# A fused two-block network on one core: the taps of a state-space batch, the phases and the attention steps placed anew

## The reference, cut to what matters

```
proj = h @ w_in[l]                       # 2048 x 6144: u, z_s, q, k, v, z_a
u, z_s, q, k, v, z_a = split(proj)
# state-space mixer: 64 groups of 16 channels, 64 complex states each
a_bar = exp(lam * step);  b_bar = ((a_bar - 1) / lam) * b_mat
bu = einsum('gnp,bsgp->bsgn', b_bar, u)
states = associative_scan(x_t = a_bar * x_(t-1) + bu_t)
y = einsum('gpn,bsgn->bsgp', c_mat, states).real + d_skip * u
y = gelu(y);  ab = y @ w_glu + b_glu;  y_s = ab[:1024] * sigmoid(ab[1024:]) * silu(z_s)
# differential attention: 8 heads of 2 maps, causal
w = softmax(q0 k0) - lam * softmax(q1 k1);  o = rms_norm(w @ v, sub_g) * (1 - lambda_init)
y_a = o * silu(z_a)
x = x + gate * (concat(y_s, y_a) @ w_out[l])
```

## Time and profile before

| what | value |
|---|---|
| median of three runs | 3105.74 us |
| the profiled execution | 3101.39 us |
| its span on the core | 3099.6 us |
| TensorE matmul, busy | 2911.4 us (94%) |
| VectorE, busy | 2148.8 us (69%) |
| ScalarE, busy | 1535.5 us (50%) |
| GpSimd, busy | 284.4 us (9%) |
| mean granted share of TensorE's clock | 0.976 |

### The profile page before, as it was taken

One profiled execution on the slowest core, in us unless ns is written; L12 is line 12 of the kernel. 1 busy time (PEld: TensorE's weight loads), 2 busy tenths in 40 slices (PEclk: granted clock), 3 DMA queues, 4 the chain that ended last, 5 costly groups with the idle time before them and its releaser, 6 DMA issues.

```text
span 3099.6 us, 59134 instructions
## 1 busy us (share of the span) xinstructions
PE 2911.4 (94%) x24112; PEld 2695.1 (87%) x24112; DVE 2148.8 (69%) x3498; ACT 1535.5 (50%) x2404; POOL 284.4 (9%) x488
## 2 busy tenths in 40 slices
PE   6899999998999999999999999999899999999987
PEld 2578777788988889999888888999899999999987
DVE  6367777687788877766665667675888746887465
ACT  3335555365555655644343434545555544555454
POOL 0012212100122220200000010010000000000000
PEclk9899999998999999999999999999999999999999
DMA  9887776884645455554333334555455555555543
GB/s 376 309 264 256 248 266 232 286 287 158 179 153 164 155 182 194 177 181 157 107 108 110 115 117 137 163 178 184 134 190 185 186 184 180 181 187 177 184 151 116
DMA packets 168223, 580.91 MB, mean 187 GB/s; under 512 B 40272, under 2 KB 40304, under 8 KB 155536
## 3 DMA queue, kind: packets, MB, share of 16 engines
q1 hardware_dynamic: 146784, 525.40, 51.1%
q0 software_dynamic: 20592, 48.26, 5.1%
q10 hardware_dynamic: 576, 3.47, 0.3%
HBM read 555.22 MB, written 21.76 MB: 186 GB/s over the span
## 4 chain that ended last, share of the span: by engine, by line
PE 68%; DVE 15%; DMA 7%; ACT 5%; issue 4%; SPq 1%; POOL 0%; DVEq 0%; ACTq 0%
PE acc L988 67%; DVE arena L948 6%; ACT arena L985 3%; DVE upper L948 2%; DVE arena L958 1%; DMA arena<-in_w_ada 1%; DMA arena<-scr_k 1%; DVE rounded L941 1%; DMA arena<-in_w_in 1%; DMA scr_k<-arena 1%; DVE upper L958 1%; PE acc L991 1%; DMA upper<-in_w_ada 1%; ACT L985 1%; ACT upper L985 1%
## 5 line engine op out<-in xcount | busy, mean ns | idle before, releaser
L988 PE MATMUL acc<-rounded 128*128 128x256 f32 x14688 | 1913.1, 289 | 33.4 <-issue 14.3
L988 PEld LDWEIGHTS acc<-rounded 128*128 128x128 f32 x14688 | 1820.8, 194 | 117.1 <-issue 88.0
L944 ACT ACTIVATE rounded<-arena 128x1024 fp32r<-128x1024 f32 x802 | 847.7, 1059 | 735.4 <-PE acc L988 554.5
L941 DVE TENSOR_TENSOR rounded<-arena,rounded 128x1024 fp32r<-128x1024 f32 x802 | 974.8, 1225 | 247.0 <-ACT rounded L944 246.7
L988 PEld LDWEIGHTS acc<-upper_rounded,rounded 128*128 128x128 f32 x4560 | 551.8, 193 | 16.2 <-issue 14.0
L988 PE MATMUL acc<-upper_rounded,rounded 128*128 128x256 f32 x4560 | 557.7, 284 | 1.4 <-DVE rounded L941 0.9
L985 ACT ACTIVATE arena<-arena 128x256 f32<-128x256 f32 (+4 forms) x477 | 251.3, 527 | 226.3 <-DVE arena L948 143.1
L948 DVE TENSOR_TENSOR arena<-arena 128x256 f32<-128x256 f32 (+5 forms) x458 | 244.0, 533 | 46.2 <-ACT arena L985 33.2
L948 DVE TENSOR_TENSOR arena<-acc,arena 128x256 f32<-128x256 f32 (+4 forms) x270 | 117.2, 434 | 222.7 <-PE acc L988 213.2
L988 PE MATMUL acc<-arena 128*32 128x512 f32 (+8 forms) x1550 | 214.5, 487 | 51.4 <-DVE arena L948 23.0
L958 DVE SCALAR_TENSOR_TENSOR arena<-arena 128x256 f32<-128x256 f32 (+6 forms) x465 | 208.1, 448 | 51.0 <-ACT arena L985 35.3
(11 more groups left out here) (94 smaller groups left out, 1260.2 us busy)
## 6 DMA issues: line engine op xcount, KB each, us to landing
arena<-in_w_in SPq DMA_DIRECT2D x328, 512.0 KB, 4.6
arena<-in_w_ada SPq DMA_DIRECT2D x88, 1024.0 KB, 5.4
arena<-in_w_up SPq DMA_DIRECT2D x176, 512.0 KB, 4.1
arena<-in_w_down SPq DMA_DIRECT2D x88, 512.0 KB, 3.9
arena<-in_w_outa SPq DMA_DIRECT2D x32, 512.0 KB, 6.7
arena<-in_w_glu SPq DMA_DIRECT2D x32, 512.0 KB, 6.2
arena<-in_w_outm SPq DMA_DIRECT2D x32, 512.0 KB, 4.6
arena<-in_w_out SPq DMA_DIRECT2D x32, 512.0 KB, 4.3
```

Source lines behind the costliest of these rows:

```text
L941: return Op(self, self.e and self.e.tensor_tensor(o, a, b, SUB), False)
L944: return Op(self, self.e and self.e.activation(o, a, ACT.Copy), False)
L988: return self.put(self.e and self.e.matmul(o, l, r, start=start, stop=stop, skip_group_check=True))
```

## The change

- `s5_prep` 4 forms the taps now, from `VV` and `CC`, after `cc`, and `s5_prep` 6 does the transposes. ScalarE copies the taps in 5 and the vectors in 7; the latter has a new wait for the product `x` of two batches before, which reads the same `VX` buffer. GpSimd's store of the taps moves from beat 7 to beat 5; its loads stay in beat 8. Waits that stood for the last user of bank 4 or of `VV` name `vx` now, where they named `ks`.
- `s5_phases`: the nine VectorE instructions come in three beats (four, three and two instructions), 8, 10 and 12 calls after the start of an odd batch, and the sines after 15. The first phases of a layer take seven calls instead of five.
- `attention`: the rests after steps 10, 11, 12 and 14 are one call longer each. A head takes 34 calls instead of 30.

No instruction is added or taken away.

```
@@ -591,11 +591,13 @@
                     yield
 
     def s5_phases(self, l, p):
-        for _ in range(10 if p else 0):
+        for _ in range(8 if p else 0):
             yield
-        self.add("s5_phase", l, p)
-        for _ in range(4):
+        for part in range(3):
+            self.add("s5_phase", l, p, part)
             yield
+            yield
+        yield
         self.add("s5_sine", l, p)
         yield
 
@@ -625,7 +627,7 @@
         for h in range(8):
             while ("w_in", l, 8 + 4 * h + 3) not in self.marks:
                 yield
-            for i, rest in enumerate((2, 2, 2, 2, 2, 2, 4, 2, 2, 2, 1, 2, 2, 2, 1)):
+            for i, rest in enumerate((2, 2, 2, 2, 2, 2, 4, 2, 2, 2, 2, 3, 3, 2, 2)):
                 self.add("att", l, h, i)
                 if i == 14:
                     self.add("part", ("att", l), h)
@@ -1159,20 +1161,17 @@
     def s5_prep(l, b, i):
         CC, VX, WI, CT, NST, ST, D0 = SETS[b % 2]
         if i == 4:
-            pe.wait_ge("s5_dve", ("vv", l, b))
-            if b:
-                pe.wait_ge("s5_act", ("ks", l, b - 1))
-            elif l:
-                pe.wait_ge("s5_act", ("ks", 0, 15))
+            pe.wait_ge("s5_dve", ("cc", l, b))
+            if b or l:
+                pe.wait_ge("s5_act", ("vx", l, b - 1) if b else ("vx", 0, 15))
+            for g in range(4):
+                x = pe.mm(B(4, 0, 128, p0=32 * g, np_=32), V(VV + g * 128, 32), V(CC + g * 144, 128), True, True)
+            x.then_inc("s5_pe", ("ks", l, b))
+        if i == 6:
+            pe.wait_ge("s5_act", ("ks", l, b))
             for g in range(4):
                 x = pe.tr(B(4, g * 128, 128), V(VV + g * 128, 128))
             x.then_inc("s5_pe", ("vx", l, b))
-        if i == 6:
-            pe.wait_ge("s5_dve", ("cc", l, b))
-            pe.wait_ge("s5_act", ("vx", l, b))
-            for g in range(4):
-                x = pe.mm(B(4, 0, 128, p0=32 * g, np_=32), V(VV + g * 128, 32), V(CC + g * 144, 128), True, True)
-            x.then_inc("s5_pe", ("ks", l, b))
 
     def s5_run(l, b, i):
         CC, VX, WI, CT, NST, ST, D0 = SETS[b % 2]
@@ -1385,7 +1384,7 @@
         return x
 
     def kk(i):
-        pe.wait_ge("s5_act", ("ks", 1, 15))
+        pe.wait_ge("s5_act", ("vx", 1, 15))
         pe.wait_ge("rw_act", ("ksq", i))
         heads(4, 2 * i, SQK + 256 * i).then_inc("rw_pe", ("ksq", i))
 
@@ -1610,13 +1609,15 @@
     def s5_prep(l, b, i):
         CC, VX, WI, CT, NST, ST, D0 = SETS[b % 2]
         if i == 5:
-            act.wait_ge("s5_pe", ("vx", l, b))
-            act.act(V(VX, 512), B(4, 0, 512), ACT.Copy).then_inc("s5_act", ("vx", l, b))
-        if i == 7:
             act.wait_ge("s5_pe", ("ks", l, b))
             if b:
                 act.wait_ge("s5_taps", (l, b - 1))
             act.act(V(KS + 112, 128), B(4, 0, 128), ACT.Copy).then_inc("s5_act", ("ks", l, b))
+        if i == 7:
+            act.wait_ge("s5_pe", ("vx", l, b))
+            if b >= 2:
+                act.wait_ge("s5_pe", ("x", l, b - 2))
+            act.act(V(VX, 512), B(4, 0, 512), ACT.Copy).then_inc("s5_act", ("vx", l, b))
 
     def s5_sine(l, p):
         both = lambda at: V(at, (CT1 - ARE, 2), (1, 128))
@@ -2087,7 +2088,7 @@
         if i == 1:
             dve.wait_ge(f"l_bc{b % 2}", (l, b))
             if b:
-                dve.wait_ge("s5_pe", ("ks", l, b - 1))
+                dve.wait_ge("s5_pe", ("vx", l, b - 1))
             for j, to in enumerate((VV, TM)):
                 dve.tt(V(to, 4, 8, 16), V(PQ + 512 * j + 8 * g0, (8, 4), (1, 8), (0, 16)), ch(BC + 64 * j, 8), MUL)
         if i == 2:
@@ -2099,16 +2100,20 @@
             dve.tt(V(TM, 4, 9, 16), pw(P2, 9), ch(BC + 192, 9), MUL)
             dve.tt(V(CC, 576), V(CC, 576), V(TM, 576), ADD).then_inc("s5_dve", ("cc", l, b))
 
-    def s5_phase(l, p):
+    def s5_phase(l, p, part):
         gap, first = CT1 - ARE, 8 * p + 4
         both = lambda at: V(at, (gap, 2), (1, 128))
         turns = lambda a: V(a + first, (-4, 2), (1, 4), (0, 32))
         chunks = lambda name: V(CON + CCOL[name], (0, 2), (0, 4), (1, 32))
-        dve.tt(V(TM, 2, 4, 32), turns(IM), chunks("c8"), MUL)
-        dve.tt(V(ARE + 384, (gap, 2), (32, 4), (1, 32)), turns(R8), chunks("cm"), MUL)
-        reduce_angle(both(ARE + 256), V(TM, 2, 128), V(TM + 256, 2, 128), 0.0)
-        dve.ts(both(ARE + 256), both(ARE + 256), PI_LO, -PI_LO, MIN, MAX)
-        dve.stt(both(ARE), both(ARE + 256), -1.0, both(ARE + 256), MUL, MAX).then_inc("s5_dve", ("ph", l, p))
+        if part == 0:
+            dve.tt(V(TM, 2, 4, 32), turns(IM), chunks("c8"), MUL)
+            dve.tt(V(ARE + 384, (gap, 2), (32, 4), (1, 32)), turns(R8), chunks("cm"), MUL)
+            turns_of(V(TM + 256, 2, 128), V(TM, 2, 128), 0.0)
+        if part == 1:
+            turned(both(ARE + 256), V(TM, 2, 128), V(TM + 256, 2, 128))
+        if part == 2:
+            dve.ts(both(ARE + 256), both(ARE + 256), PI_LO, -PI_LO, MIN, MAX)
+            dve.stt(both(ARE), both(ARE + 256), -1.0, both(ARE + 256), MUL, MAX).then_inc("s5_dve", ("ph", l, p))
 
     def s5_run(l, b, i):
         CC, VX, WI, CT, NST, ST, D0 = SETS[b % 2]
@@ -2500,7 +2505,7 @@
         if i == 3 and b < 14:
             pool.wait_ge("s5_dve", ("cc", l, b))
             bc(l, b + 2)
-        if i == 7:
+        if i == 5:
             pool.wait_ge("s5_act", ("ks", l, b))
             if b >= 2:
                 pool.wait_ge("s5_pe", ("y", l, b - 2))
```

More of the change, by code:

```diff
@@ L1169, in s5_prep @@
             x.then_inc("s5_pe", ("vx", l, b))
[L1170 to L1175, removed]
     def s5_run(l, b, i):
```

5 lines of the change are left out of this document (1 added, 4 removed).

## The result

The changed kernel took 3113.72 us, the median of 20 runs (3106.66 to 3117.60), beside 3105.35 for the kernel before (20 runs, 3097.72 to 3117.01) on the same chips: a ratio of 1.0026, 95% interval 1.0018 to 1.0034, that is 8.4 us slower. The forecast was 3095.7 and its range ended at 3108.0. The profiled execution took 3109.77 us, its span is 3108.0, 8.4 above that of before, so the two traces can be laid side by side.

A forecast was written before the change was run, and what follows sets the result against it. TensorE, busy 94% of the span, was taken as the bound, leaving 48 us idle in the two large projections. Terms -10.5 + 4.3 - 8 - 0.8 + 0.7 - 3 + 6 + 1.3 = -10.0 gave 3095.7 us, range 3083 to 3108.

The forecast's parts named there:

- Taps' waits: TensorE's seven waits for the taps' landing (scr_k) in both layers go: -10.5 us, bounds 0 to 10.8.
- Vectors' late copy: ScalarE's vectors' copy, now nearer the next batch's first product, makes that product wait: +4.3 us, bounds 0 to 6.2.
- Phases: Splitting VectorE's nine instructions removes waits at row maxima, sines and transposes behind them: -8 us, bounds 0 to 14.
- The boundary: Between the layers, TensorE's 5.99 us wait behind the sine and its table load falls to near 3.3.
- - 0.8 + 0.7: First phases' extra turns: -0.8 us net at the layers' boundary, +0.7 at layer 0's start, before the first product.
- Attention steps: Transposes' waits for scaled rows shrink, -3 us; late head 7's copy behind the tanh delays its product, +6, bounds 0 to 10.
- The clock has no part: In both layers' large projections the clock is at its upper level (0.99 and 0.98), so it was given no part.
- Given back: Sooner TensorE meets ScalarE's waits for weights in layer 0 more often: +1.3 us, bounds 0 to 10.
- rival A: Waits return elsewhere as VectorE, ScalarE and weights set the pace: give-back 7, time 3101.4; chance 0.13.
- the sign that I named: ScalarE's waits for weights growing past 96 us, with TensorE behind them.
- Idle time in the two stretches: TensorE's idle time in both layers' large projections, forecast near 38 us instead of 48.
- Rival C: Head 7's copy behind the tanh costs its full 10, later steps also meet gelu steps; 24 lost, 3114 us; chance 0.11.

The follow-up runs named there:

- Parts 1 and 2: The taps and transposes swap plus the phases in three beats, without the attention rests, against the kernel before: 0.9971, 3095.78 us.
- the drift alone: Kernel before with only the last attention rest four turns longer, so a head takes 34 turns with inner spacing untouched: 1.0140, 3147.77 us.
- Parts 1 and 2 with two rests: Taps swap and three-beat phases, plus rests after attention steps 10 and 12 one call longer, head of 32 turns, against the kernel before: 0.9952, 3088.68 us.

## Why the prediction was wrong, by its own steps

- **Taps' waits, -10.5: right.** No TensorE wait names scr_k after the change; 10.8 us are gone.
- **Vectors' late copy, +4.3: right for the swap, wrong for the whole.** Alone it cost 6.7 - 2.9 = 3.8 us. In the full change the first product waits 13.2, +10.3. With the phases added to the swap it is 11.4, and with the rests alone, without any swap, 11.5; 6.1 of the 13.2 are batch 14's two waits behind late head 7's exponentials. The other edits too make ScalarE late for this product, and I had priced each edit against the old order of the others.
- **Phases, -8: the named waits went, 5 us in the time when alone.** In the two layers ScalarE has no wait at a sine but one of 1.1 us, and the waits of the earlier trace rows are gone. So are the two of 2.73 and 3.62 us at head 7's product, which I had put into the bounds only (ahead of the second ScalarE stood 0.99 us at its sine, a third such wait beside my two). But in the trace of this edit alone the idle time of that part fell by 0.2 us and not by 8. The boundary, forecast near 3.3, reads 3.15 in the kernel after (answers to the earlier trace rows):

```profile
735.39 0.80 PE L990 MATMUL acc<-arena 128*128 128x1 f32 x4 [3.15 <-DVE arena L950]
```

- **Parts 1 and 2 as a sum: near the edge.** -10.5 + 4.3 - 8 - 0.8 + 0.7 + 1.3 = -13.0; measured -9, interval -5 to -13.
- **Attention steps, -3 and +6: the step that failed.** Measured +17 on top of the rest, +24 alone. The gain itself was better than said: the waits of `att` 13 went from 7.2 us to 0. The wait at head 7's product came where and as large as forecast (3.00 in layer 0, 3.02 in layer 1, 6 together; parts 1 and 2 have none there, the kernel before 6.3). Two things were priced at zero. One is what else stands late with the heads: I followed only head 7's copy to the tanh, not its exponentials, which now stand ahead of batch 14's copy and make its first product wait 2.48 and 3.66 us, and not the earlier heads (head 3's transposes wait 5.3 us, 3.9 more than with parts 1 and 2). The other is the clock.
- **"The clock has no part": wrong.** It had none in the rows that I read, 0.99 and 0.98 over 360 us; those are means of before. TensorE's busy time rose 9.8 us for the same work, and that is more than the whole loss. In idle time alone, the change was a small gain of 1.4 us, and the sum of -10.0 was 8.6 us off; the other 9.8 were nowhere in it. (Taps alone and phases alone are busy 2916.0 and 2917.7, 4.6 and 6.3 above before, though the two layers have only 47.8 and 51.2 us at the lower clock. Over the whole trace they have 176.2 and 176.5 us at it, the kernel before 152.0 and the full change 183.0: the profiled execution of the kernel before had little low clock outside the two layers, so the busy times of two single executions can differ by some 5 us for no reason of the edit.)
- **Given back, +1.3: too small where it can be read.** Up to the end of layer 1's large projection the idle time fell by 2.1 us with the taps alone and by 0.2 with the phases alone, where I had 6 and 8; with both it fell by 10.2, where I had 13. This is rival A's effect in part, but not by the sign that I named: ScalarE's waits for in_w_in are shorter after the change (answers to the earlier trace rows):

```profile
ACT rounded L946 <- DMA arena<-in_w_in: 60.4, 22, 9.2
```

- **Idle time in the two stretches:** forecast 38 us, measured 18.8 + 29.0 = 47.8 by the two rows above, as before.
- **Rival C had the time (3114 against 3113.7) and the place,** head 7's copy behind the tanh; undoing that one meeting brings the change to 0.9987. That the time agrees within 1 us is luck. Its reason was half: it asked for 24 us of waits at this copy and the steps behind it, and the traces show 6 us of waits there and 6 at batch 14's first product, with about as much again by the low clock. Its chance of 0.11 rested on the wait alone. Had I priced a wait in this stretch at twice its length, my 6 would have been 12 and the sum -4, and with batch 14's 6.1 us at the same price +8. That is hindsight, and other terms were off as well.

What stays open: how the price of the two meetings divides. Undoing the one at the tanh gives back 12 us (6 to 19) of the 17; no kernel undid only the one at the exponentials, or held the clock up after that first wait. Open too is why the drift alone costs 43 us and the rests alone 24, when the rests in the full change cost 17: the wider spacing, the taps and the phases seem to spare heads 1 to 6 much of it, and which head is spared by which edit was not tried.

## What to carry to other kernels

In a program whose engines walk one list, a chain of steps that repeats with a fixed stream must not outlast its period: check the sum of its rests first (34 turns against 32 here), since two turns per head are harmless in the first head and land somewhere else in each later one. When a late step is followed to what it meets, follow every step of that chain, also those that make others wait. Widen rests by the calls that are spare (30 to 32 here) and take none from another rest: of two ways to 32 turns, the one that did gave 0.9991, the one that didn't 0.9952. And when a stall of some 3 us appears in a stretch where TensorE is nearly always busy, price it at up to twice its length (3.0 us cost 4.6 and 5.5 here), and look at the busy time for the same number of matmuls beside the idle time.

## What the hardware showed that I had not expected

- A wait of 3.66 us in a stretch that is 92% busy (331.04 of 360 us) went with the lower clock (0.77 from 1110 to 1120), and one of 3.02 us, some 13 us later, with another fall (0.66 from 1120 to 1130); five products of constants in place of most of the second wait kept the same 10 us at 1.00. The Trainium skill (TensorE: Matmul & The Clock Gate, "HAM oscillation — how this bites in real kernels") describes such a clock that falls with each wait for data, in a kernel of short bursts; this trace agrees, and shows it with isolated waits in dense work too.
- Not every wait costs that. In the kernel before, six matmuls behind head 7's wait took 0.96 us in layer 0 (wait 2.73) and 1.63 in layer 1 (wait 3.62). Parts 1 and 2 with two rests have 12.4 us less idle time than before, but 54.6 us at the lower clock in the two layers against 47.8; parts 1 and 2 alone have 41.0. Over the runs here, idle time and low clock go together only roughly, and what decides it beside a wait's length is not shown.
- A later head alone changed no instruction and cost 43 us, 25 of them idle time and 18 in TensorE's busy time: the largest effect of all kernels here came from the smallest edit.
